# The start of a diffusion block: first norm from the token rows, first modulations with the weight block as stationary operand

## The reference

```
sh_a, sc_a, ga_a, sh_f, sc_f, ga_f = split(silu(c) @ w_mod + b_mod, 6)     # latent tokens
tsh_a, tsc_a, ...                  = split(silu(c_ctx) @ w_mod + b_mod, 6) # context tokens
h  = rms_norm(x,  g_attn) * (1 + sc_a)  + sh_a
ht = rms_norm(xt, g_attn) * (1 + tsc_a) + tsh_a
... = split_mixer_inputs(h @ w_in), split_mixer_inputs(ht @ w_in)   # q, k, v of three head groups
```

## Time and profile before

| what | value |
|---|---|
| median of 3 runs | 1742.12 us (1742.0 to 1745.38) |
| the profiled execution: time, span | 1742.0 us, 1742.0 us |
| PE busy | 1646.7 us, 95% |
| DVE, ACT, POOL busy | 1067.4, 755.4, 782.5 us |
| beginning, up to the end of `dense_pair` | 74.7 us |

### The profile page before, as it was taken

How to read it: one execution, slowest core, us unless ns; L and a number is a source line. 1 busy time by engine, 2 the same in 40 slices (tenths; PEclk the granted TensorE clock), 3 DMA queues, 4 the chain that set the end, 5 groups by cost and what they waited for, 6 DMA issues and landing times.

```text
span 1742.0 us, 28585 instructions
## 1 busy us (share of the span) xinstructions
PE 1646.7 (95%) x11013; PEld 1124.4 (65%) x11013; DVE 1067.4 (61%) x2071; ACT 755.4 (43%) x1364; POOL 782.5 (45%) x576
## 2 busy tenths in 40 slices
PE   7999989988989999999999999997988999999998
PEld 3688878966856666666666667886776644444444
DVE  4534499995468884688449845457995625426334
ACT  3222268875243431234323323226875365356342
POOL 2244436662524444335433343551334657557563
PEclk9999999999999999999999999999999999999999
DMA  9345453312125423253326232554003233243222
GB/s 326 48 122 140 122 142 83 104 51 81 41 73 163 140 67 116 75 180 109 122 73 206 91 67 54 138 130 110 15 1 94 77 106 100 85 126 92 73 85 85
DMA packets 317285, 179.17 MB, mean 103 GB/s; under 512 B 88526, under 2 KB 310494, under 8 KB 317150
## 3 DMA queue, kind: packets, MB, share of 16 engines
q1 hardware_dynamic: 284542, 143.63, 30.0%
q10 hardware_dynamic: 32608, 33.71, 6.0%
HBM read 158.97 MB, written 2.83 MB: 93 GB/s over the span
## 4 chain that ended last, share of the span: by engine, by line
PE 70%; DVE 18%; issue 4%; ACT 4%; DMA 2%; SPq 1%; POOL 1%; ACTq 0%; DVEq 0%; POOLq 0%
PE acc L950 58%; DVE mod_acc L2122 4%; DVE stat L1914 3%; DVE prob_t L1928 2%; PE side L1139 1%; PE mod_ps L1055 1%; PE acc L1122 1%; DVE o_sum L1940 1%; PE acc L1123 1%; PE small L1154 1%; PE small L898 1%; PE side L885 1%; ACT prob_t L1507 1%; DVE act L1748 1%; PE mod_ps L1139 1%
## 5 line engine op out<-in xcount | busy, mean ns | idle before, releaser
L950 PE MATMUL acc<-act,pair_w 128*128 128x512 f16 x3168 | 578.8, 344 | 7.1 <-ACT act L1371 3.5
L950 PEld LDWEIGHTS acc<-act,pair_w 128*128 128x128 f16 x3168 | 308.2, 98 | 266.7 <-issue 9.1
L950 PE MATMUL acc<-act,split_w 128*128 128x512 f32 (+1 forms) x1920 | 378.0, 354 | 9.0 <-DVE act L2054 4.4
L950 PEld LDWEIGHTS acc<-act,split_w 128*128 128x128 f32 x1920 | 307.8, 189 | 61.7 <-DVE act L2054 6.9
L800 POOL TENSOR_SCALAR pair_raw<-pair_raw,weight_scale 128x1024 f32<-128x1024 f32 x88 | 108.9, 1237 | 325.6 <-ACT pair_w L1556 325.6
L950 PE MATMUL acc<-hidden,down_w 128*128 128x512 f16 (+1 forms) x1056 | 247.8, 343 | 1.6 <-DVE hidden L2088 0.8
L2122 DVE SCALAR_TENSOR_TENSOR mod_acc<-mod_chunk,silu_c,mod_acc 128x256 f32<-128x256 f32 x280 | 196.4, 744 | 4.0
L803 POOL TENSOR_TENSOR pair_w<-pair_raw,pair_w 128x1024 f16<-128x1024 f32 x88 | 192.3, 2185 | 7.3
L692 POOL TENSOR_SCALAR split_w<-raw_w 128x1024 fp32r<-128x1024 f32 x72 | 77.5, 1076 | 257.6 <-PE acc L950 161.2
L695 POOL TENSOR_TENSOR split_w<-raw_w,split_w 128x1024 fp32r<-128x1024 f32 x72 | 173.6, 2411 | 6.0
L2083 DVE SCALAR_TENSOR_TENSOR prod<-acc,prod_scale,silu_g 128x768 f32<-128x768 f32 (+1 forms) x44 | 38.9, 884 | 207.2 <-PE acc L950 198.2
(11 more groups left out here) (223 smaller groups left out, 2396.2 us busy)
## 6 DMA issues: line engine op xcount, KB each, us to landing
mod_chunk<-in_w_mod ACTq DMA_DIRECT2D x28, 1024.0 KB, 5.0
pair_raw<-in_w_gate SPq DMA_DIRECT2D x44, 512.0 KB, 3.8
pair_raw<-in_w_up SPq DMA_DIRECT2D x44, 512.0 KB, 4.9
raw_w<-in_w_in SPq DMA_DIRECT2D x64, 256.0 KB, 3.7
raw_w<-in_w_mod SPq DMA_DIRECT2D x24, 512.0 KB, 4.1
raw_w<-in_w_down SPq DMA_DIRECT2D x20, 512.0 KB, 4.2
mod_start<-in_w_mod SPq DMA_DIRECT2D x8, 1024.0 KB, 10.7
ks<-q_split SPq DMA_DIRECT2D x64, 96.0 KB, 2.4
```

What stands on the lines that cost most here:

```text
L950: mm = pe.matmul(acc[slot][:, a:b], own, moving[:, part == 1, k, a:b], start=(k == 0 and part == 0), stop=(k == n - 1 and part == 1))
```

## The change

There are two parts.

1. The squares. ACT takes the squares straight from the landed token tiles (`square_tokens`): six instructions over 1024 features, whose accumulator gives the sum of each token in `norm_inv`. The squares of `x_t`, DVE's six additions and PE's sums with the column of ones are gone for this norm. PE no longer waits for the small vectors before the tokens, the transposes go round three PSUM tiles (`acc[0]`, `acc[1]`, `side`), and DVE copies six of the eight tiles, ACT k = 2 and 5. SP's load of start block 3 also waits for the last square.
2. The first modulations. The 128x128 weight piece is the stationary operand and the two conditions are the moving one: 4 pieces of the block by 8 k are 32 matmuls of 2 columns, whose results lie along features at once. `take_rows` and `turn_first_modulations` are gone. Blocks use two PSUM banks in turn (`first_ps`), block 1 comes after `spread_inverse`, block 2 ahead of tile k = 2 and block 3 ahead of tile k = 4.

The diff, cut to its core:

```diff
+        first_ps = [mod_ps, small]
         turned_at = [side[:, 0:512], side[:, 512:1024], mod_ps[:, :]]
...
             sp.dma_start(columns[:, :, :], k_columns[:, :, :]).then_inc(consts_in, 16)
             sp.dma_start(sinks[:, :], bass.AP(sink.tensor, 0, [[0, P], [1, DEPTH * 6]])).then_inc(consts_in, 16)
             sp.wait_ge(xt_ps, KT)
+            sp.wait_ge(ssq_tok, TOK // P)
             load_start(N_START - 1)
...
         @block.tensor
         def _(pe):
+            def tokens_to_features(k):
+
+                if k >= 3:
+                    before = k - 3
+                    if before % 3 == 2:
+                        pe.wait_ge(xt_act, before // 3 + 1)
+                    else:
+                        pe.wait_ge(xt_dve, before - before // 3 + 1)
+                for t in range(6):
+                    if k == 0 and t == LAT // P:
+                        pe.wait_ge(ctx_in, 16)
+                    mm = pe.transpose((acc[0], acc[1], side)[k % 3][:, P * t:P * t + P], tokens[:, t, P * k:P * k + P], ident[:, :])
+                mm.then_inc(xt_ps, 1)
+
+            pe.wait_ge(ident_in, 16)
+            pe.wait_ge(x_in, 16)
+            tokens_to_features(0)
+            tokens_to_features(1)
             pe.wait_ge(vecs_in, N_VECS * 16)
-            pe.wait_ge(ident_in, 16)
             pe.transpose(small[:, 0:P], rows_v[:, :], ident[:, :])
             pe.transpose(small[:, P:P + N_ROWS], rows_c[:, :], ident[0:N_ROWS, 0:N_ROWS]).then_inc(vec_ps, 1)
-
-            pe.wait_ge(x_in, 16)
-            pe.wait_ge(ctx_in, 16)
-            for k in range(KT):
-                if k >= 2:
-                    pe.wait_ge(xt_act if k % 2 == 0 else xt_dve, k // 2)
-                for t in range(6):
-                    mm = pe.transpose(acc[k % 2][:, P * t:P * t + P], tokens[:, t, P * k:P * k + P], ident[:, :])
-                mm.then_inc(xt_ps, 1)
-
+            for k in range(2, KT):
+                tokens_to_features(k)
+
+            pe.wait_ge(xt_act, 2)
             pe.wait_ge(rows_ready, 1)
...
             def first_modulations(i):
                 pe.wait_ge(mod_start_in[i], 32)
-                if i == 1:
-                    pe.wait_ge(xt_dve, KT // 2)
-                elif i:
-                    pe.wait_ge(mod_rows_ready, i - 1 if i == 2 else i)
-                ps = acc[1][0:2, 512:1024] if i == 1 else small[0:2, :]
-                for k in range(KT):
-                    mm = pe.matmul(ps, silu_c[:, k::KT], mod_start[i][:, k, :],
-                                   start=(k == 0), stop=(k == KT - 1))
-                mm.then_inc(mod_start_done, 1)
-
-            def turn_first_modulations(i):
-
-                pe.wait_ge(mod_rows_ready, i + 1)
-                if i:
-                    pe.wait_ge(mod_ready, i)
+                if i >= 2:
+                    pe.wait_ge(mod_ready, i - 1)
                 for a in range(2 * START_TILES):
-                    mm = pe.transpose(mod_ps[:, 2 * a:2 * a + 2], mod_rows[:, 512 * i + P * a:512 * i + P * a + P], ident[0:2, 0:2])
+                    for k in range(KT):
+                        mm = pe.matmul(first_ps[i % 2][:, 2 * a:2 * a + 2], mod_start[i][:, k, P * a:P * a + P], silu_c[:, k::KT],
+                                       start=(k == 0), stop=(k == KT - 1))
                 mm.then_inc(mod_first, 1)
...
+                if nu == 0:
+                    pe.wait_ge(scale_ready, 1)
                 pe.wait_ge(inv_ready, nu + 1)
...
                     pe.wait_ge(silu_c_ready, 1)
                     pe.wait_ge(vec_ready, 1)
                     first_modulations(0)
-                    first_modulations(1)
-                if l == 0:
-                    sum_first_squares(0, TOK)
-                sum_squares(2 * l, TOK)
-                if l == 0:
-                    turn_first_modulations(0)
+                else:
+                    sum_squares(2 * l, TOK)
                 spread_inverse(2 * l, TOK)
                 if l == 0:
-                    turn_first_modulations(1)
-                    first_modulations(2)
+                    first_modulations(1)
                 def in_tile(k):
-                    if l == 0 and k == 1:
-                        turn_first_modulations(2)
-                    if l == 0 and k == 4:
-                        first_modulations(3)
-                        turn_first_modulations(3)
+                    if l == 0 and k in (2, 4):
+                        first_modulations(1 + k // 2)
                     pe.wait_ge(h_hi, 2 * l * KT + k + 1)
...
                 sc.dma_start(rows_v[r + 56:r + 64, :], norm_ffn[l].rearrange("(k p) -> k p", p=P)).then_inc(vecs_in, 16)
+            def square_tokens(t):
+
+                sc.activation(squares_tok[:, :], tokens[:, t, :], ACT.Square, accum_out=norm_inv[:, t:t + 1]).then_inc(ssq_tok, 1)
+
+            sc.wait_ge(x_in, 16)
+            for t in range(LAT // P):
+                if t:
+                    sc.wait_ge(ssq_tok, t)
+                square_tokens(t)
             sc.wait_ge(vec_ready, 1)
             sc.activation(silu_c[:, :], vecs[:, P:P + 2 * KT], ACT.Silu).then_inc(silu_c_ready, 1)
-            for k in range(0, KT, 2):
+            sc.wait_ge(ctx_in, 16)
+            for t in range(LAT // P, TOK // P):
+                k = 2 + 3 * (t - LAT // P)
                 sc.wait_ge(xt_ps, k + 1)
-                sc.activation(x_t[:, k, :], acc[0][:, 0:TOK], ACT.Copy).then_inc(xt_act, 1)
+                sc.activation(x_t[:, k, :], side[:, 0:TOK], ACT.Copy).then_inc(xt_act, 1)
+                sc.wait_ge(ssq_tok, t)
+                square_tokens(t)
...
             def take_norm_root(nu, w):
-                sc.wait_ge(ssq_done, nu + 1)
                 if nu:
+                    sc.wait_ge(ssq_done, nu)
                     sc.wait_ge(inv_ready, nu)
-                sc.activation(norm_root[:, 0:w // P], side[:, TOK:TOK + w // P], ACT.Sqrt, bias=eps[:, 0:1],
-                              scale=1.0 / D).then_inc(root_ready, 1)
-
-            def shifted(nu, l, w, ahead=None):
+                else:
+                    sc.wait_ge(ssq_tok, TOK // P)
+                sums = side[:, TOK:TOK + w // P] if nu else norm_inv[:, :]
+                sc.activation(norm_root[:, 0:w // P], sums, ACT.Sqrt, bias=eps[:, 0:1], scale=1.0 / D).then_inc(root_ready, 1)
+
...
                     sc.wait_ge(filled, 2)
                 sc.activation(root_first[:, :], eps[:, 0:1], ACT.Sqrt)
-                squares(2 * l, TOK, ready, last_downs if l else None)
-
-                def take_rows(i):
-                    sc.wait_ge(mod_start_done, i + 1)
-                    src = acc[1][0:2, 512:1024] if i == 1 else small[0:2, :]
-                    sc.activation(mod_rows[:, 512 * i:512 * i + 512], src, ACT.Copy).then_inc(mod_rows_ready, 1)
-
-                if l == 0:
-                    take_rows(0)
-                    take_rows(1)
+                if l:
+                    squares(2 * l, TOK, ready, last_downs)
                 take_norm_root(2 * l, TOK)
-                shifted(2 * l, l, TOK, lambda k: take_rows({3: 2, 6: 3}[k]) if l == 0 and k in (3, 6) else None)
+                shifted(2 * l, l, TOK)
...
             ve.tensor_scalar(rows_s[:, :], ones[0:N_ROWS, :], row_max[0:N_ROWS, 2:3], None, ALU.mult).then_inc(rows_ready, 1)
-            for k in range(1, KT, 2):
+            for k in range(KT):
+                if k % 3 == 2:
+                    continue
                 ve.wait_ge(xt_ps, k + 1)
-                ve.tensor_copy(x_t[:, k, :], acc[1][:, 0:TOK]).then_inc(xt_dve, 1)
+                ve.tensor_copy(x_t[:, k, :], acc[k % 3][:, 0:TOK]).then_inc(xt_dve, 1)
...
                 k0, k1 = START_TILES * i, START_TILES * (i + 1)
                 b = vecs[:, 0:MOD_FIRST].rearrange("p (s k a) -> p s k a", s=2, a=1)[:, :, k0:k1, :].broadcast_to((P, 2, START_TILES, 2))
-                ps = mod_ps[:, 0:4 * START_TILES].rearrange("p (s k a) -> p s k a", **two)
+                ps = first_ps[i % 2][:, 0:4 * START_TILES].rearrange("p (s k a) -> p s k a", **two)
                 ve.tensor_tensor(mod[:, 0, 0:MOD_FIRST, :].rearrange("p (s k) a -> p s k a", s=2)[:, :, k0:k1, :], ps, b,
...
-
-            for k in range(1, KT - 1):
-                add_square(0, k, TOK)
...
```

More of the change, by code:

```diff
@@ L1076, in _ @@
                         elif l == 0:
-                            pe.wait_ge(xt_act, 4)
-                            pe.wait_ge(xt_dve, 4)
+                            pe.wait_ge(xt_act, KT // 3)
+                            pe.wait_ge(xt_dve, KT - KT // 3)
                         else:
@@ L1338, in squares @@
                             sc.wait_ge(q_normed, N_QK * (nu // 2 + 1))
-                        elif nu:
+                        else:
                             sc.wait_ge(scaled_ready, nu * KT)
                     elif k >= 3:
-                        sc.wait_ge(ssq_part, nu * N_ADD + k - 2)
+                        sc.wait_ge(ssq_part, (nu - 1) * N_ADD + k - 2)
```

(29 more changed lines are left out.)

18 lines of the change are left out of this document (8 added, 10 removed).

## The result

| | before | change |
|---|---|---|
| median | 1742.06 us (1741.82 to 1745.38, 4 runs) | 1757.88 us (1754.65 to 1765.63, 4 runs) |
| ratio, 95% interval | | 1.0093 (1.0069 to 1.0117) |
| span of the profiled execution | 1742.0 us | 1756.1 us |
| L1034 before, L1029 after (the dense pair is done) | 74.7 us | 90.7 us |

The change makes the kernel 0.9% slower, 15.8 us by the medians; the forecast's sum was 1757.1. One thing in the table ahead has to be put right. Of the change the profiled execution has a time of 1757.93 us and a span of 1756.1, and every run of the experiments shows the same 1.8 us between the two. So the profiled execution of before, with its span of 1742.0, will have had a time near 1743.8 (an estimate from those), not 1742.0. If the 1742.0 among the four times of before is this span, their median would be near 1743.0 and the loss 14.9 us, also an estimate.

What follows compares the result with a forecast made beforehand. PE was taken to bound the kernel, with 70% of the chain. Start, blocks, spread, dense passes and low-clock loss, 21.5 + 4 x 11.0 + 2.8 + 17.3 + 4.2, gave 89.8 us against 74.7, so 1757.1 us; range 1745 to 1768.

Steps and rivals of the forecast that it cites:

- The start of block 0: First modulation block on PE: starts at 21.5 us instead of 20.6, +0.9 (between 0 and +2), with ACT's squares hidden.
- The blocks: Four first modulation blocks of 64 two-column passes: 6.7 us each at full clock, 13.6 at low, 11.0 taken.
- The step that carried most: Block 0: clock falls 3.2 us after the last dense pass, so 30 passes at 0.105 and 34 at 0.213, 10.4 us.
- Spread and dense passes: Spread of the inverse 2.8 us; 96 dense passes 17.3 us, plus 4.2 lost as three groups start at low clock.
- Sum and carry: Dense pair ends at 89.8 us against 74.7; the 15.1 us shift is carried whole to the end, 1757.1 us.
- The base of the sum: Whole kernel before: profiled execution of 1742.0 us and median of 1742.12 taken for one.
- The clock holds: Rival for the blocks: gaps, not few columns, lower the clock; blocks cost 6.7 us, 7.2 less, 1734.8; chance 0.11.
- The low clock spares weight loads: Rival for the blocks: about 6.8 us each at either clock; only dense passes and spread pay, 1740.3; chance 0.03.
- The clock falls late: Rival for the blocks: 5.3 us until each fall is the rule; slower by little, 1742 to 1746; chance 0.05.
- The squares do not leave the path: Rival before block 0: slower squares or delayed silu start it later, 3 us on ACT being 3 on PE; 1760; chance 0.04.
- the low end: Stretch to the dense pair's end with the low terms, 21.5 + 36 + 1.9 + 17.3 + 1 = 77.7 us, so 1745.
- the first rival: Clock stays full through the modulation blocks: 6.7 us each, spread 1.8, dense pair done at 67.5, 1734.8; chance 0.11.

Runs made afterwards that it cites:

- cols64: The change with the two condition columns repeated to 64 moving columns in the first modulations; median 1737.49 us, 0.9967 of the kernel before.
- sq_only: The change with only its squares part, the first modulations as in the kernel before; median 1736.93 us, 0.9967 of the kernel before.
- cols48: The change with the two condition columns repeated to 48 moving columns in the first modulations; median 1748.82 us, 1.0033 of the kernel before.
- the second set: The change timed again without an edit, beside later experiments; median 1762.41 us, 1.0103 of the kernel before.
- cols64_sq6: cols64 with the last token tile squared six more times on ACT ahead of its own square; median 1746.93 us, 1.0012 of the kernel before.
- cols128: The change with the two condition columns repeated to 128 moving columns in the first modulations; median 1738.27 us, 0.9965 of the kernel before.
- cols16: The change with the two condition columns repeated to 16 moving columns in the first modulations; median 1751.81 us, 1.0077 of the kernel before.
- mods128_only: The kernel before with only the new first modulations, moving columns repeated to 128, squares as before; median 1748.09 us, 1.0027 of the kernel before.
- cols128_sq6: cols128 with the last token tile squared six more times on ACT ahead of its own square; median 1737.94 us, 0.9968 of the kernel before.

## Why the prediction was right

**The start of block 0**, 21.5 us: 21.37. That this is so close is luck: in the kernels with the same program ahead of it, block 0 starts anywhere from 20.15 (`cols64`, `sq_only`) to 21.96 (`cols48`). ACT's squares take some 1.2 us each with the read of the accumulator (1.06 and 0.19 us, overlapping a little), not 1.05, and the last one ends at 21.84 where 21.4 was said; the inverse is there at 23.76 (23.4 said). Hidden, as stated. The wait of PE on DVE's six copies is in the row of 16.35 (0.83 us).

**The blocks**, 11.0 each, 44.0 together: 9.36, 13.51, 10.84 and 10.49 from start to start, 44.2. The price at the low clock, 0.213, held: block 1 gives 0.211. The one at the full clock was a little low: in block 0 the passes start 0.112 us apart until the fall (42 of them in 4.7 us), so a block would cost 7.1 us and not 6.7; in the twelve passes of the earlier trace rows the first interval is short. The step that carried most, how many passes fall into the low clock, was chosen by two falls in the profile of before; it came out on the sum and not block by block, which is luck: in block 0 the clock fell later than supposed (9.36 us against 10.4), and block 1 got no clock back from the spread, as the earlier trace rows had let hope, and cost 13.51.

**Spread and dense passes**, 2.8 and 21.5: 2.70 and 3.58 + 5.84 + 13.05 = 22.5. Against 0.178 us a pass the first group lost 1.4 us, the second 2.6 and the third 1.3; 1.4 had been taken for each.

**Sum and carry.** The sum was 89.8 and the mark is at 90.7. That a shift would be carried whole was a little too strong: 14.1 us of 16.0 arrive at the end of the span. The base of the sum was 1.8 us too low, by the time of the profiled execution. With the 0.9 us at the mark the errors nearly cancel, which is why 1757.1 lies so close to 1757.88. That is luck: the runs of the change themselves go from 1752.6 to 1766.04, and the second set gave a median of 1762.41. What held is the mechanism, narrow passes that lower the clock and then pay for it, and its size.

**The rivals.** *The clock holds*: false for the change. Where it was made to hold, the price is near: the rival had 7.2 us less, and `cols64` has its mark 7.7 earlier, with blocks dearer than the rival's (7.1 us against 6.7) and an earlier start of block 0 (20.15 against 21.5). Its mechanism, that gaps lower the clock, is half true: the clock fell in a gap in `cols64_sq6`, but in the change no gap stands ahead of the fall at 26 us. The rule of the Trainium skill ("TensorE: Matmul & The Clock Gate", section "Why this matters for your kernels") names idle gaps between bursts of matmuls; that section says nothing of a fall during work without a gap, which is what the change's trace has. *The low clock spares weight loads*: false. In `cols64_sq6` the same 64 passes with the same kind of load cost 13.75 us at 0.50 (block 1) and 7.25 at 1.00 (block 2). The load time by columns alone that the Trainium skill gives ("TensorE: Matmul & The Clock Gate", section "LDWEIGHTS (loading the stationary operand)") does not hold at the low clock here: passes that each load 128 columns start 0.213 us apart. *The clock falls late*: it did fall late in block 0 (0.61 on average from 25 to 30 us puts the fall near 26.1, 4.7 us in), but it did not come back for block 1. *The squares do not leave the path*: false, with a cover of 5 us and more.

**What was mis-sized** without harm: the spread at the full clock, 1.82 us from start to start, is 1.34 to 1.54 (`cols128`, `sq_only`). It came from a row that straddled a fall of the clock. The forecast's sum took the 2.8 of the low clock instead; the low end, the first rival and the expectation for `cols128`, which missed, used it.

## What to carry to other kernels

Price a TensorE pass at both clocks, and look in the profile for what lowers the clock, before a stream of wide passes is exchanged for many narrow ones with large weight loads. In this kernel the narrow form with its moving columns repeated to 64 or 128 costs 7.3 us a block against 7.0 for the wide form, and saves the turn; either, together with the squares on ScalarE, gives a kernel about 0.3% faster than before. With 64 columns the clock was lost when PE had to wait for 2.28 us. A duration for a price is to be read from a row that lies wholly in one state of the clock.

## What the runs showed that was not expected

- Repeating the moving columns, work that nobody reads, turns a loss into a gain: ratios to before of 0.9967 (0.9955 to 0.9979) with 64 columns and 0.9965 (0.9955 to 0.9975) with 128, where the change has 1.0093 (1.0069 to 1.0117).
- Keeping the clock and getting it back differ: at 1.00 the blocks of `cols64` kept it, while block 1 of `cols64_sq6`, at 0.50, stayed there for 13.75 us. Blocks of 16 and of 128 columns did get it back at that place (`cols16`, `mods128_only`). These are single profiles, and what decides it is open.
- Passes with 128x128 float32 weights take the same time with 2, 64 and 128 moving columns, 0.112 us each from start to start at the full clock.
- The first token transposes run at half pace, though the recorded clock is 1.00. Six of them take 1.54 us at 13.97 in the change, as in `sq_only`, and later in `sq_only` six take this:

```profile
17.92 0.82 PE L855 MATMUL side<-ident,tokens 128*128 128x128 f32 x6
```

In every trace they start 0.213 us apart at first and 0.109 us apart later, the ratio of the two clock levels. The step has come by 16.3 us in `sq_only` and comes near 19.3 in the change, whose program is the same up to there, and this is what moves the start of block 0. The likely reading, not tested, is that PE starts at the low level and the record does not have it; so a recorded 1.00 at the very start should be checked against the pace.

Left open: why `cols64`, `cols128`, `cols128_sq6` and `sq_only`, whose marks lie between 67.0 and 71.1, all have medians within 1.4 us of each other. They ran on different chips, the start of block 0 moves by up to 1.8 us from one execution to another, and the clock falls at other places later on; no run here separates these.
